# Projection in five equal groups of 416 tokens instead of four of 512 and one of 32

## The reference, cut to what matters

```python
def mix_project(h, w_in_l):
    p = jnp.einsum('btd,de->bte', h, w_in_l)
    qa, ka, va, qb, kb, vb = jnp.split(p, np.cumsum(PROJ_SIZES)[:-1].tolist(), axis=-1)
    ...
h = rms_norm(xp, norm_mix_pre[l])               # 2048 prompt tokens
qa, ka, va, qb, kb, vb = mix_project(h, w_in[l])
...
h = rms_norm(xs, norm_mix_pre[l])               # 32 sample tokens
qa, ka, va, qb, kb, vb = mix_project(h, w_in[l])
```

## Time and profile before

| | us |
|---|---|
| median of three runs | 3973.7 |
| the profiled execution | 3991.15 |
| span of its trace | 3989.6 |
| projection in that trace, first to last matmul | about 642 |
| TensorE busy in the span | 3464.0 (87%) |

### The profile page before, as it was taken

The page is one execution under the profiler, slowest core; times in us unless marked ns, Lnnn a source line. Parts: engine busy times, 40 slices in busy tenths (PEclk is TensorE's granted clock), DMA queues, the critical chain, the costliest instruction groups (busy, mean ns, idle before and its releaser), DMA issues. The chain is left out here.

```text
span 3989.6 us, 56296 instructions
## 1 busy us (share of the span) xinstructions
PE 3464.0 (87%) x18718; PEld 2892.7 (73%) x18718; DVE 1779.8 (45%) x4182; ACT 1212.3 (30%) x2563; POOL 694.9 (17%) x459
## 2 busy tenths in 40 slices
PE   6999999388878997387679699999999999999994
PEld 5888888377768997244468488778877887788883
DVE  5121212266656665132179355336534652455422
ACT  4111111255555554122145232232223222322211
POOL 0000000288870000133145100000001000100001
PEclk7999999699999999699789799999999999999997
DMA  4334333724416666799378645436644654444221
GB/s 127 99 96 106 97 99 95 155 50 86 96 32 152 160 153 151 236 329 331 109 224 250 184 147 189 145 103 193 196 125 120 194 172 133 122 137 142 90 72 48
DMA packets 584274, 573.07 MB, mean 144 GB/s; under 512 B 43369, under 2 KB 483522, under 8 KB 578178
## 3 DMA queue, kind: packets, MB, share of 16 engines
q1 hardware_dynamic: 559012, 437.26, 40.1%
q0 software_dynamic: 19680, 65.42, 5.1%
q10 hardware_dynamic: 5408, 68.23, 5.0%
HBM read 468.37 MB, written 169.68 MB: 160 GB/s over the span
## 5 line engine op out<-in xcount | busy, mean ns | idle before, releaser
L2213 DVE TENSOR_TENSOR ff_wl<-ff_wr,ff_wh 128x1024 fp32r<-128x1024 f32 (+2 forms) x304 | 331.7, 1091 | 698.8 <-ACT ff_wh L2124 698.8
L2124 ACT ACTIVATE ff_wh<-ff_wr 128x1024 fp32r<-128x1024 f32 (+2 forms) x304 | 287.1, 945 | 911.7 <-PE ff_d L2047 301.7
L426 PE MATMUL pj_acc<-hT_h,pj_wh 128*128 128x512 f32 (+1 forms) x960 | 355.8, 371 | 10.8 <-POOL pj_wl L344 10.7
L426 PE MATMUL pj_acc<-hT_l,pj_wh 128*128 128x512 f32 (+1 forms) x960 | 326.8, 367 | 0.0
L2014 POOL TENSOR_TENSOR ff_yn<-ff_yn,ff_xt 128x1024 f32<-128x1024 f32 x16 | 42.1, 2634 | 1624.5 <-DVE ff_yn L2303 1563.9
L2045 PE MATMUL ff_g<-ff_hh,ff_wh 128*128 128x512 f32 x704 | 294.9, 419 | 34.7 <-issue 14.9
L2045 PE MATMUL ff_d<-ff_ah,ff_wh 128*128 128x512 f32 x704 | 296.0, 420 | 16.8 <-DVE ff_al L2256 11.9
L2045 PE MATMUL ff_u<-ff_hh,ff_wh 128*128 128x512 f32 x704 | 289.8, 412 | 0.0
L2046 PE MATMUL ff_g<-ff_hh,ff_wh 128*128 128x512 f32 x704 | 278.3, 395 | 0.0
L2046 PE MATMUL ff_d<-ff_al,ff_wh 128*128 128x512 f32 x704 | 277.9, 395 | 0.0
L2047 PE MATMUL ff_g<-ff_hh,ff_wl 128*128 128x512 f32 x704 | 277.3, 394 | 0.0
(11 more groups left out here) (273 smaller groups left out, 7000.9 us busy)
## 6 DMA issues: line engine op xcount, KB each, us to landing
ff_wr<-in_w_gate SPq DMA_DIRECT2D x88, 512.0 KB, 3.8
ff_wr<-in_w_up SPq DMA_DIRECT2D x88, 512.0 KB, 5.1
sa_vca<-in_cache_a_v POOLq DMA_DIRECT2D x128, 256.0 KB, 8.2
sa_kca<-in_cache_a_k SPq DMA_DIRECT2D x128, 256.0 KB, 13.8
out<-in_cache_win_k ACTq DMA_DIRECT2D x64, 511.0 KB, 4.3
out<-in_cache_win_v ACTq DMA_DIRECT2D x64, 511.0 KB, 4.4
ff_wr<-in_w_down SPq DMA_DIRECT2D x64, 384.0 KB, 3.3
ab_qq<-scratch_qT SPq DMA_DIRECT2D x40, 512.0 KB, 11.8
```

What stands on the lines that cost most here:

```text
L426: m = pe.matmul(acc[g][:, 0:width(g)], weights[:, k, c], part[:, c, cols], start=start, stop=stop)
L2124: act.activation(wh[:, slot % 2, 0:size], wr[:, slot, 0:size], ACT.Copy).then_inc(w_hi, 1)
L2213: dve.tensor_tensor(wl[:, slot % 2, 0:size], wr[:, slot, 0:size], wh[:, slot % 2, 0:size].bitcast(F32), ALU.subtract).then_inc(w_lo, 1)
```

## The change

The tokens are cut into five groups of 416 (`PG` = 2080 / 5). Group 4 has the last 384 prompt tokens and the 32 sample tokens. The first pass takes groups 0, 1 and 2 and the second groups 3 and 4. The split now runs over all five groups, with its two buffers taken in turn over the whole list of splits (`slot`); of the last group only the 384 prompt tokens are split (`prompt`). Turning still works on blocks of 128 tokens, so a turn waits for the last copied group that its tokens reach into (`covering`). The order on VectorE and in the sync queue follows the new passes.

```diff
+PG = TOK // NAT
...
-        qh = s.sb("qh", [P, 2, GRP], F32R)
-        ql = s.sb("ql", [P, 2, GRP], F32R)
+        qh = s.sb("qh", [P, 2, PG], F32R)
+        ql = s.sb("ql", [P, 2, PG], F32R)
...
-        SPLIT = [NAT * u + g for u in range(NU) if PROJ[u][1] != "v" for g in range(NG)]
+        SPLIT = [NAT * u + g for u in range(NU) if PROJ[u][1] != "v" for g in range(NAT)]
...
+        def prompt(g):
+            return min((g + 1) * PG, SEQ) - g * PG
+        def covering(g):
+            return (min((g + 1) * GRP, TOK) - 1) // PG
+        def slot(g, u):
+            return nth(SPLIT, NAT * u + g) % 2
...
+                k, w = slot(g, u), prompt(g)
                 for part, src in enumerate((qh, ql)):
-                    sp.dma_start(first[kind][part][ds(4 * (u // 3) + j, 1)][0][:, g * GRP:(g + 1) * GRP],
-                                 src[:, g % 2].bitcast(F32)).then_inc(qk_out[g % 2], 16)
+                    sp.dma_start(first[kind][part][ds(4 * (u // 3) + j, 1)][0][:, g * PG:g * PG + w],
+                                 src[:, k, 0:w].bitcast(F32)).then_inc(qk_out[k], 16)
...
-                        act.activation(st[:, u % 2, g * GRP:g * GRP + width(g)], acc[g][:, 0:width(g)], ACT.Copy,
+                        act.activation(st[:, u % 2, g * PG:(g + 1) * PG], acc[g][:, 0:PG], ACT.Copy,
...
-                                m = pe.matmul(acc[g][:, 0:width(g)], weights[:, k, c], part[:, c, cols],
+                                m = pe.matmul(acc[g][:, 0:PG], weights[:, k, c], part[:, c, cols],
...
-                pe.wait_ge(ev, raised(NAT * (NU * j + u) + g + 1 + NAT))
+                pe.wait_ge(ev, raised(NAT * (NU * j + u) + covering(g) + 1 + NAT))
...
-                    products(n, u, (0, 1))
+                    products(n, u, (0, 1, 2))
...
-                    products(n, u, (2, 3, 4))
+                    products(n, u, (3, 4))
```

More of the change, by code:

```diff
@@ L275, in project @@
         first = {"q": t["qT"], "k": t["kT"]}
-        def width(g):
-            return GRP if g < NG else NS
+        def prompt(g):
[4 more added lines that the diff above has]
+            return nth(SPLIT, NAT * u + g) % 2
         @block.sync
@@ L319, in _ @@
                             rows_out(j, u - 1, g)
-                    for pair in ((0, 1), (2, 3)):
+                    for part in ((0, 1, 2), (3, 4)):
                         if kind != "v":
-                            for g in pair:
+                            for g in part:
                                 split_out(j, u, g)
-                        if kind != "q" and pair == (0, 1):
-                            for g in pair:
+                        if kind != "q" and part[0] == 0:
+                            for g in (0, 1):
                                 rows_out(j, u, g)
                     if kind != "v":
-                        sp.wait_ge(ev, raised(NAT * (NU * j + u) + NG + 1 + NAT))
+                        sp.wait_ge(ev, raised(NAT * (NU * j + u) + NAT + NAT))
                         sp.sem_inc(passed, 1)
@@ L362, in _ @@
                     n = NU * j + u
-                    act.wait_ge(qk_lo, raised(done(SPLIT, SIZE, j, NAT * (u - 2) + NG)))
+                    act.wait_ge(qk_lo, raised(done(SPLIT, SIZE, j, NAT * (u - 2) + NAT - 1)))
                     act.wait_ge(turned, raised(done(TURN, SIZE, j, NAT * (u - 2) + NG)))
@@ L380, in split @@
                 dve.wait_ge(ev, raised(NAT * (NU * j + u) + g + 1 + NAT))
-                dve.wait_ge(qk_out[g % 2], raised(32 * (len(SPLIT) // 2 * j + r // 2)))
-                src = st[:, u % 2, g * GRP:(g + 1) * GRP]
-                dve.tensor_copy(qh[:, g % 2], src).then_inc(qk_hi, 1)
+                k, w = slot(g, u), prompt(g)
+                dve.wait_ge(qk_out[k], raised(32 * (len(SPLIT) // 2 * j + r // 2)))
+                src = st[:, u % 2, g * PG:g * PG + w]
+                dve.tensor_copy(qh[:, k, 0:w], src).then_inc(qk_hi, 1)
                 dve.wait_ge(qk_hi, raised(len(SPLIT) * j + r + 1))
-                dve.tensor_tensor(ql[:, g % 2], src, qh[:, g % 2].bitcast(F32), ALU.subtract).then_inc(qk_lo, 1)
+                dve.tensor_tensor(ql[:, k, 0:w], src, qh[:, k, 0:w].bitcast(F32), ALU.subtract).then_inc(qk_lo, 1)
             def rows(j, u, g):
@@ L402, in _ @@
                             rows(j, u - 1, g)
-                    for pair in ((0, 1), (2, 3)):
+                    for part in ((0, 1, 2), (3, 4)):
                         if PROJ[u][1] != "v":
-                            for g in pair:
+                            for g in part:
                                 split(j, u, g)
-                        if PROJ[u][1] != "q" and pair == (0, 1):
-                            for g in pair:
+                        if PROJ[u][1] != "q" and part[0] == 0:
+                            for g in (0, 1):
                                 rows(j, u, g)
@@ L421, in products @@
                         for g in groups:
-                            cols = slice(g * GRP, g * GRP + width(g))
+                            cols = slice(g * PG, (g + 1) * PG)
                             for part in parts:
```

## The result

The kernel after took 3933.52 us (median of six runs, 3926.21 to 3944.35), beside 3978.82 for the kernel before (six runs, 3970.95 to 3989.96). The ratio is 0.9887, 95% interval 0.9866 to 0.9908: 45 us less, between 37 and 53. The profiled execution took 3931.5 us, its span is 3930.0 against 3989.6.

What follows compares the result with a forecast made beforehand. The projection was taken to be bound by TensorE's matmul stream. Savings of 50.9 us in the stream and 0.5 at the end, 51.4 together, off 3973.7 gave 3922.3 us; range 3915 to 3933, widened to 3909 to 3937.

Steps and rivals of the forecast that it cites:

- The bound: Projection: the stage is as long as TensorE's matmul stream, busy 635.65 of 643 us, and nothing feeds TensorE late.
- The old chunk and the 0.116 us of a short product: Projection before: a chunk takes 1.7275 + 1.380 = 3.1075 us, its three 32-column products 0.116 us each.
- The price of 416 columns: Projection's products after: 0.1895 us each, 2.8425 us a chunk of all five groups, saving 50.9 us.
- Where it comes from: Projection: short products paid about 0.11 us for a weight load whatever their width, and now hide it.
- The covers: Projection: turning, next unit's weights, copies, fifth split, stores and turned copies cost TensorE 0 us.
- The cover over the weights: Next unit's weights: a 4.5 us chain, covered by the 9.1 us second pass with 4.6 us left, cost 0.
- The end: Projection's end: two last pieces of at most 416 columns are split and stored, 0.5 us saved.
- The start: Projection's start: the time at the low clock level does not depend on width; 0, at most 1 us either way.
- "The stages behind it should keep their lengths": Stages after the projection: lengths unchanged in the trace after.
- The straight line: Projection: time per product linear from 32 to 512 columns, 0.207 us at 416, so no gain, 3974 us; chance 0.03.
- the slot of the drawn load: Projection: each product takes its weight load's slot, 0.230 us whatever streams, +65.8 us, 4039 us; chance 0.03.
- the stores as well: Projection: stores of split pieces hold VectorE and, through turned copies, TensorE; 27 us lost, 3949 us; chance 0.04.

Runs made afterwards that it cites:

- Experiment 2: Kernel before with 18 of the 24 32-column sample-group products of each unit left out: 3930.35 us, ratio 0.9882.
- Experiments 1: Kernel before with the sample group's products 224 columns wide instead of 32: 3978.58 us beside 3977.35, ratio 1.0001.
- 4: Kernel after with most products cut to 416, 352, 288, 224, 160 or 96 columns by unit, projection incomplete: 3839.35 us in one run.
- 3: Kernel after with groups of 512, 512, 512, 272 and 272 tokens instead of five of 416: 3939.82 us, ratio 0.9924.
- 5: Kernel after with its passes back at groups 0-1 and then 2-3-4, VectorE and sync queue to match: 3943.36 us, ratio 0.9910.
- experiment 12: Kernel after with the next unit's weights rounded after the copy of group 4 instead of group 1: 4092.59 us in one run.
- experiments 7 to 10: Kernel before with 20 one-column VectorE fills: ratio 1.0029; kernel after with 40: 0.9867; kernel after again, unpadded 0.9887, with 40 fills 0.9863.
- the kernel with 40 fills: Kernel after with 40 one-column VectorE fills ahead of the projection's loop, run twice: 3926.21 us (ratio 0.9867) and 3921.59 us (0.9863).
- 6: Kernel after with one buffer instead of two for the split pieces: 3940.87 us, ratio 0.9900.

## Why the prediction was right, and where it was not

- **The bound.** Right: the stage followed TensorE's stream, and its waits did not move.
- **The old chunk and the 0.116 us of a short product.** Right. Experiment 2 has 0.1155.
- **The price of 416 columns.** Forecast 0.1895 us, measured 0.188 in first passes and 0.190 in second ones, 0.1887 over both. The term was 0.0008 too large. The stream lost 54.8 us (642.1 to 587.3) where I had 50.9. Of the 3.9 us between, 15 x 192 x 0.0008 = 2.3 are this term; 192 x 0.0025 = 0.5 are the old chunk, 3.110 us in the mean of 23 units where my two samples gave 3.1075; and about 1.1 are the start, below. Interpolating between 384 and 512 alone gave 0.1888, and I had moved away from it.
- **Where it comes from.** Right and shown: the level at 0.112 us. Experiments 1 and 4 show it flat to 224 columns, 3 that five unequal groups above it have the same stream, and 5 that the passes bring none of it.
- **The covers.** The turning, the weights, the fifth split and the stores cost TensorE nothing, as said. The stores landed sooner than before, in 2.5 us for 208 KB where I had allowed 4.1. The cover over the weights was priced as the wait alone, "TensorE would stand still once in each unit"; it would also lose its clock (experiment 12).
- **The end.** Forecast -0.5 us; from the last matmul's end to the next stage 10.45 us before and 9.0 after, -1.4.
- **The start.** Held to about 1 us. The first matmul came 0.7 us later, but matmuls ran at the low level for 6.2 us before (66.73 to 72.9) and for 4.0 after (67.41 to 71.4); half of the difference, 1.1 us, is in the stream's gain. Over all traces this stretch lasts 5.2 to 6.1 us with the old cut of the tokens and 2.9 to 6.0 with the new one, so it is not shown to be the change's.
- **"The stages behind it should keep their lengths".** Wrong, and it is the reason that the runs gained 45 us and not the 56 of the stage. I had counted VectorE's fifth split as work, and not as 20 more instructions in its program (80 more executed in the four turns of the loop). They move everything behind them, and attention B's loop came to lie where each of its three turns stalls twice. That costs 9 to 12 us (experiments 7 to 10). The sum had no term for it.
- **The sum.** The runs gained 3978.8 - 3933.5 = 45.3 us. The stage's 56.2 less attention B's 12.4 are 43.8. The two profiled executions differ by more, 59.6 us, because the one before was among the slowest of its kernel; attention A and the samples' attention differ in them too, by -7.6 and -11, but over the traces of all versions they lie between 464 and 477 and between 367 and 384 us, and the ranges of the versions overlap; I did not pursue them, so that 43.8 and 45.3 come so close is not shown to be more than chance. The measured 3933.5 us is 11.2 above the forecast of 3922.3: 5.1 of it because the kernel before came out at 3978.8 instead of 3973.7, and 6.1 because the gain was smaller. That is outside the forecast's own 3915 to 3933, by under 1 us, and inside only since I had widened it to 3937. The range held partly by luck: nothing in it was meant for attention B, and 4.8 us more from the projection paid for a part of what attention B took. Without the second stall the forecast is met: the kernel with 40 fills took 3926.21 and 3921.59 us.
- **The rivals.** The straight line is out (1, 4), the slot of the drawn load too (loads drawn 0.19 us long follow every 0.11 us), and the stores as well (6). What the Trainium skill's page "TensorE: Matmul & The Clock Gate" gives as sustained spacings in "Back-to-back issue gap", 81 ns at 128 columns and 131 at 512, was not what this kernel shows: 112 ns up to 224 columns and 231 at 512, and no straight line between. Its advice of 512 or more in every dimension, in "Why this matters for your kernels", decides nothing here: the old cut breaks it with its group of 32, the new one with all five groups, and three groups of 512 with two of 272 have the stream of five of 416 (experiment 3).

**What stays open.** That VectorE's second stall depends on where its instructions lie in the program is shown from both sides. That the reason is a fetch of the program rests on the packets of queue 14: 25 of them in attention B in all eight traces with second stalls and 21 in the six without, one inside nearly every stall, and VectorE going on at a steady distance behind it. The trace doesn't say for which engine a packet of that queue is, and no run shows how the program is cut into pieces, so where a second stall will come can't be computed from what is shown here. The first stall, 3.4 us or more, was there in every version, at two or three of the turns.

## What to carry to other kernels

A matmul with a weight load of its own has a least price, here 0.112 us, whatever it streams. Where a rest of a few columns is its own group, cut the groups so that none is under that (here about 240 columns, between 224 and 272); above it, equal and unequal groups had the same stream in the one pair tried. And when the trace says that the changed stage gained more than the program, compare the stages behind it for "issue" waits at the turns of their loops, and move the program by a few instructions before looking for a deeper reason.

## What was not expected

- 20 added instructions that compute nothing, in a stage where the engine is idle, make the program 11 us longer; 40 in another version make it 8 to 13 us shorter.
- Waits of 3.9 us in TensorE's stream, once a unit, cost 55 us on top of their own 90, by the clock that TensorE lost behind them.
- The drawn length of a weight load, 0.19 us at the 2.4 GHz level, is the same at every pitch from 0.11 to 0.23. So PEld's busy share misleads as a bound: it rose from 527.58 of 643 us before to 567.84 of 588 after, though loads held the short products before and hold none after.
